# Attention output kept in channel layout: transposes replaced by a transfer between partitions, row sums spread as a factor, three near rows

## The reference, cut to what matters

```
logits = einsum('bqhgd,bqkhd->bqhgk', qg, k_sel) * HEAD_DIM**-0.5 + bias   # only selected keys
p = softmax(logits)
o = einsum('bqhgk,bqkhd->bqhgd', p, v_sel)
y_a = (o * silu(g_attn)) @ w_attn_out
```

## Time and profile before

| what | us |
|---|---|
| median of 3 runs | 3389.51 |
| lowest and highest run | 3388.55, 3389.98 |
| the profiled execution's own time | 3395.7 |
| its span, first to last instruction | 3394.0 |
| attention stage, first full step to last product | 894.9 |

### The profile page before, as it was taken

One profiled execution on the slowest core, in us unless ns is written; L12 is line 12 of the kernel. 1 busy time (PEld: TensorE's weight loads), 2 busy tenths in 40 slices (PEclk: granted clock), 3 DMA queues, 4 the chain that ended last, 5 costly groups with the idle time before them and its releaser, 6 DMA issues. The chain is left out here.

```text
span 3394.0 us, 50403 instructions
## 1 busy us (share of the span) xinstructions
PE 3245.1 (96%) x19461; PEld 2999.2 (88%) x19461; DVE 2697.9 (79%) x4071; ACT 1467.3 (43%) x1961; POOL 1038.4 (31%) x888
## 2 busy tenths in 40 slices
PE   7999999999999999999998999999999989899998
PEld 4999888999999999999997887787777879899987
DVE  2542788898989999999995999999999965875444
ACT  2322566988930200001002776676767740432121
POOL 3222111543335300000002453444533324674200
PEclk9999998999999999999998999999999999999999
DMA  6465535445555643344445323223222245577343
GB/s 236 131 190 165 155 100 141 158 149 187 185 180 178 256 177 138 138 162 170 159 144 145 78 59 81 75 57 99 59 60 61 60 154 199 159 236 257 127 143 114
DMA packets 381524, 485.53 MB, mean 143 GB/s; under 512 B 49296, under 2 KB 304464, under 8 KB 379685
## 3 DMA queue, kind: packets, MB, share of 16 engines
q1 hardware_dynamic: 325605, 287.14, 28.2%
q10 hardware_dynamic: 44352, 149.49, 12.4%
q0 software_dynamic: 11392, 46.68, 3.5%
HBM read 301.98 MB, written 184.13 MB: 143 GB/s over the span
## 5 line engine op out<-in xcount | busy, mean ns | idle before, releaser
L1140 PE MATMUL psum<-ha,gt 128*128 128x352 f32 x8136 | 1352.8, 324 | 7.7 <-DVE ha L1414 4.4
L1140 PEld LDWEIGHTS psum<-ha,gt 128*128 128x128 f32 x8136 | 1323.0, 189 | 11.6 <-DVE ha L1414 4.7
L1450 DVE SCALAR_TENSOR_TENSOR cv<-cv,vecs,cv 128x1056 f32<-128x1056 f32 (+1 forms) x480 | 607.7, 1342 | 0.0
L1942 ACT CAST at<-psum 128x1024 fp32r<-128x1024 f32 (+2 forms) x308 | 289.5, 940 | 265.2 <-PE psum L1853 263.4
L2016 DVE TENSOR_TENSOR at<-psum,at 128x1024 fp32r<-128x1024 f32 (+2 forms) x308 | 346.7, 1126 | 6.3 <-ACT at L1942 5.8
L717 PE MATMUL psum<-br,br 128*128 128x352 f32 x2016 | 337.1, 328 | 15.0 <-DVE br L2389 10.5
L1853 PE MATMUL psum<-ident,at 128*128 128x128 f32 (+1 forms) x2320 | 344.6, 272 | 6.0 <-DVE at L2016 4.8
L717 PEld LDWEIGHTS psum<-br,br 128*128 128x128 f32 x2016 | 330.4, 190 | 19.4 <-issue 11.8
L1271 ACT ACTIVATE gt<-psum 128x1056 f32<-128x1056 f32 x80 | 84.0, 1050 | 600.3 <-PE psum L1140 600.3
L791 DVE TENSOR_SCALAR_CACHE_REDUCE gl<-gt,gl 128x1792 bf16<-128x1792 f32 (+8 forms) x263 | 337.7, 1350 | 1.2
L1872 PE MATMUL psum<-at,at 128*128 128x512 f32 (+1 forms) x1160 | 327.2, 391 | 7.4 <-ACT at L1950 7.3
(11 more groups left out here) (255 smaller groups left out, 4142.7 us busy)
## 6 DMA issues: line engine op xcount, KB each, us to landing
scratch_ws<-gt SPq DMA_DIRECT2D x112, 512.0 KB, 4.0
gt<-scratch_ws ACTq DMA_DIRECT2D x110, 512.0 KB, 5.0
gt<-in_w_in_dram SPq DMA_DIRECT2D x60, 512.0 KB, 5.8
scratch_gm<-gt ACTq DMA_DIRECT2D x32, 528.0 KB, 3.0
br<-scratch_gm ACTq DMA_DIRECT2D x32, 528.0 KB, 3.7
scratch_m<-br POOLq DMA_DIRECT2D x32, 528.0 KB, 5.1
at<-scratch_q SPq DMA_DIRECT2D x128, 128.0 KB, 2.9
scratch_u<-gl POOLq DMA_DIRECT2D x16, 528.0 KB, 4.2
```

Of the source, the lines that this page charges most:

```text
L1140: return nc.tensor.matmul(of[:, j, 0:W // 3], part[:, c, :], a[:, c, j * (W // 3):(j + 1) * (W // 3)], start=(c == 0 and k == 0), stop=(c ...
L1450: ins = nc.vector.scalar_tensor_tensor(to[:, 0:width], mine[:, k_:k_ + width], tap, to[:, 0:width], ALU.mult, ALU.add)
L1942: nc.scalar.copy(phi[j % 3][:, 0:len(mine), 0:n], turned[j % 2][:, 0:len(mine), 0:n]).then_inc(s_phi, 1)
```

## The change

The output never leaves the channel layout. ScalarE copies the accumulator as before. A transfer brings the other 64 partitions beside the unit's own side (units alternate between the lower and the upper half), and GpSimd adds the two halves there (`fold`). The reciprocals of the row sums go out to memory as a row and come back broadcast to 64 partitions (`total_row`, `spread`); GpSimd multiplies them into the gate, reading them at a stride of four (`gain`). VectorE makes one multiplication of the two (`finish`), and SyncE stores from the accumulator's copy. TensorE's six transposes per unit and VectorE's three instructions are gone, and the ring holds score chunks alone. GpSimd walks the steps now, has three near rows instead of two (each with its mask part copied) and splits the queries of the next unit after the fourth near row; gates have four buffers.

```diff
+        self.total_at = at(self.first)
+        self.spread_at = at([n + 2 for n in self.first])
+        self.gain_at = at([n + 4 for n in self.first])
+        self.move_at = at([n + self.LAG + 1 for n in self.last])
+        self.fold_at = at([n + self.LAG + 2 for n in self.last])
+        self.out_at = at([n + self.LAG + 4 for n in self.last])
-        self.rows_at = at([n + self.LAG + 1 for n in self.last])
-        self.cols_at = at([n + self.LAG + 2 for n in self.last])
...
+        for e in range(GROUP * count):
+            self.near_at[ends[e - self.NEARS] if e >= self.NEARS else self.begin].append((e // GROUP, e % GROUP))
...
# SyncE
+            def total_row(u):
+                n = plan.queries(u)
+                sp.wait_ge(s_total, u + 1)
+                sp.dma_start(scr["ri"][u, 0:GROUP * n].rearrange("(q h) -> q h", h=GROUP), rinv[0:n, u % 4, :]).then_inc(s_row[u % 2], 16)
+            def move(u):
+                n = GROUP * plan.queries(u)
+                sp.wait_ge(s_acc, u + 1)
+                if u >= 2:
+                    sp.wait_ge(s_fold, u - 1)
+                sp.dma_start(moved[side(u), 0:n], accs[u % 2][side(u + 1), 0:n]).then_inc(s_move[u % 2], 16)
+            def spread(u):
+                n = GROUP * plan.queries(u)
+                sp.wait_ge(s_row[u % 2], 16 * (u // 2 + 1))
+                if u >= 2:
+                    sp.wait_ge(s_gain, u - 1)
+                sp.dma_start(wide[side(u), 0:n], scr["ri"][u:u + 1, 0:n].to_broadcast([HD, n])).then_inc(s_wide[u % 2], 16)
...
# GpSimd
+            def near_row(u, h):
...
+                if e >= plan.NEARS:
+                    pool.wait_ge(s_ring, plan.final(*divmod(e - plan.NEARS, GROUP)) + 1)
+                row = near[e % plan.NEARS]
+                if width > n:
+                    nc.gpsimd.tensor_copy(row[:, 0:width - n], mine[:, o:o + width - n])
+                nc.gpsimd.tensor_tensor(row[:, width - n:width], bias[g % 2][:, h, c0:c0 + n],
+                                        mine[:, o + width - n:o + width], ALU.add).then_inc(s_near, 1)
+            def settled(s, u, folds, gains):
+                if u % 2:
+                    pool.wait_ge(s_near, plan.nears_before[s])
+                    pool.wait_ge(s_query, 2 * min(plan.nears_before[s] // GROUP + 1, len(units)))
+                    pool.wait_ge(s_fold, folds)
+                    pool.wait_ge(s_gain, gains)
+            def gain(s, u):
+                n = plan.queries(u)
+                settled(s, u, plan.folds_by[s], u)
+                pool.wait_ge(s_ga[u % plan.GATES], 16 * (u // plan.GATES + 1))
+                pool.wait_ge(s_wide[u % 2], 16 * (u // 2 + 1))
+                nc.gpsimd.tensor_tensor(gate(u), gate(u), wide[side(u), 0:GROUP * n].rearrange("d (q h) -> d h q", h=GROUP),
+                                        ALU.mult).then_inc(s_gain, 1)
+            def fold(s, u):
+                n = GROUP * plan.queries(u)
+                settled(s, u, u, plan.gains_by[s - 1])
+                pool.wait_ge(s_move[u % 2], 16 * (u // 2 + 1))
+                nc.gpsimd.tensor_tensor(folded(u), folded(u), moved[side(u), 0:n], ALU.add).then_inc(s_fold, 1)
...
+            for s in plan.steps:
+                for u in plan.fold_at[s]:
+                    fold(s, u)
+                for u in plan.gain_at[s]:
+                    gain(s, u)
+                for u, h in plan.near_at[s]:
...
+                    near_row(u, h)
+                    if h == GROUP - 1 and u + 1 < len(units):
+                        queries(u + 1)
...
# ScalarE, ahead of the accumulator's copy
-                        act.wait_ge(s_rp, plan.slot[("rows", u - 2)] + 1)
+                        act.wait_ge(s_st[u % 2], 16 * (u // 2))
# VectorE (rows and columns removed here, as on TensorE)
+            def totals(u):
+                n = plan.queries(u)
+                dve.wait_ge(s_exp, GROUP * (u + 1))
...
+                nc.vector.reciprocal(rinv[0:n, u % 4, :], total[0:n, u % plan.SUMS, :]).then_inc(s_total, 1)
+            def finish(u):
+                dve.wait_ge(s_gain, u + 1)
+                dve.wait_ge(s_fold, u + 1)
+                mine = folded(u).rearrange("d (h t) -> d h t", h=GROUP)
+                nc.vector.tensor_tensor(mine, mine, gate(u), ALU.mult).then_inc(s_out, 1)
```

More of the change, by code:

```diff
@@ L1465 @@
     SUMS = 6
+    NEARS = 3
+    GATES = 4
     TILES = [t for k in range(NT // 2) for t in (k, NT - 1 - k)] + [NT]
@@ L1514, in __init__ @@
             seen += 1
-        self.end = len(self.pairs) + self.LAG + 4
+        self.end = len(self.pairs) + self.LAG + 5
         self.steps = range(self.begin, self.end)
@@ L1533, in __init__ @@
         for s in self.steps:
-            for key in ([("max",) + x for x in self.chunks_at[s]] + [("rows", u) for u in self.rows_at[s]]
-                        + [("cols", u) for u in self.cols_at[s]]):
-                self.slot[key] = len(self.slot)
+            for x in self.chunks_at[s]:
+                self.slot[("max",) + x] = len(self.slot)
     def queries(self, u):
@@ L1616, in attention_stage, with side, gate, folded @@
         block = ctx.enter_context(nc.Block())
+        def side(u):
+            return slice((u % 2) * HD, (u % 2 + 1) * HD)
+        def gate(u):
+            return ga[u // 2 % 2][side(u), :, 0:plan.queries(u)]
+        def folded(u):
+            return accs[u % 2][side(u), 0:GROUP * plan.queries(u)]
         def bank(key):
@@ L1715, in _ @@
                         queries(u)
+                for u in plan.move_at[s]:
+                    move(u)
+                for u in plan.spread_at[s]:
+                    spread(u)
+                for u in plan.total_at[s]:
+                    total_row(u)
                 for u in plan.store_at[s]:
@@ L1786, in nears @@
                 o = keys_of(t)[1] - width
[L1787 to L1800, removed]
@@ L1807, in _ @@
                               10: lambda g, k: keys_high(g, k, 1), 11: lambda g, k: keys_low(g, k, 1), 12: group_high}
-            for u in range(2, len(units)):
-                queries(u)
-                nears(u, parts_of_group.get(u % NTL) if u // NTL + 1 < KV else None)
+            queries(0)
+            for s in plan.steps:
[4 more added lines that the diff above has]
+                for u, h in plan.near_at[s]:
+                    if h == 2 and u % NTL in parts_of_group and u // NTL + 1 < KV:
+                        parts_of_group[u % NTL](u // NTL + 1, u % NTL)
+                    near_row(u, h)
+                    if h == GROUP - 1 and u + 1 < len(units):
+                        queries(u + 1)
+                        if u == 0:
+                            values_low(0)
@@ L1875, in values @@
                     last.then_inc(s_pv, 1)
[L1877 to L1893, removed]
             pe.wait_ge(s_set, SET)
@@ L1910, in _ @@
                     scores(*todo.pop(0))
[L1911 to L1914, removed]
         @block.scalar
@@ L1975, in masked @@
                     dve.wait_ge(s_near, GROUP * u + h + 1)
-                    other = near[h % 2][0:n, 0:w]
+                    other = near[(GROUP * u + h) % plan.NEARS][0:n, 0:w]
                 else:
@@ L2017, in _ @@
                                             phi[j % 3][:, 0:len(mine), 0:n].bitcast(F32), ALU.subtract).then_inc(s_plo, 1)
[L2018 to L2021, removed]
+                for u in plan.total_at[s]:
+                    totals(u)
+                for u in plan.out_at[s]:
+                    finish(u)
 def branch_stage(nc, mem, x, w, out, scr):
```

86 lines of the change are left out of this document (40 added, 46 removed).

## The result

The changed kernel takes 3344.0 us as the median of 4 runs (3341.4 to 3348.7), against 3389.7 before: a ratio of 0.9858, 95% interval 0.9841 to 0.9875. The forecast was 3343.

What follows compares the result with a forecast made beforehand. TensorE and VectorE, both nearly full, bound the 894.9 us attention stage. VectorE's 784 us plus 64 idle gives 848: -47, tail +0.5, so 3349 from the profiled 3395.7; runs' median 6.2 us lower: 3343. Range 3314 to 3372.

Steps and rivals of the forecast that it cites:

- Two engines side by side: Attention stage, 894.9 us: TensorE busy 851.4 and VectorE 830.9, each handing the other work in every step.
- The sum's last step: Stage time: of TensorE's count, 828 us, and VectorE's, 848 us, the larger governs, giving -47 us.
- VectorE's sum: VectorE's busy time in the attention stage: 830.9 - 110 + 63 = 784 us, plus 64 us idle.
- The part put on: New VectorE multiplication per unit: 0.688 us plus 0.27 us waiting for GpSimd, 63 us for the stage.
- the remark that most cases meet no wait: VectorE's multiplication at L1997 in the kernel before: its median, 0.426 us, shows most cases do not wait for GpSimd.
- TensorE's 48 us: Six transposes for each of 68 units leave TensorE, saving 48 us; 19.5 us of waits behind L1997 go too.
- The rival in which TensorE governs: Attention stage: VectorE's idle time shrinks as TensorE's work gets shorter, giving 3315 to 3323 us; chance 0.14.
- The near rows: GpSimd's row buffers in the attention stage: the third covers its new waits at fold time, a step and a half.
- The move: 128 KB SBUF-to-SBUF transfer before the fold: 0.36 + 2.3 = 2.7 us, just covered by a 2.9 us step.
- The sums' way: Row sums out to memory and broadcast back: two steps, 5.8 us, per leg; 16-byte pieces up to 6.6 us; cost zero.
- The blocked multiplication: Rival: the new VectorE multiplication waits out GpSimd instructions, 3370 to 3414 us, deciding from 1.62 us each; chance 0.09.
- The tail: End of the attention stage, last copy through fold and multiplication to last store: 0.5 us later.

Runs made afterwards that it cites:

- the dead loads: Changed kernel with work nobody reads put back per unit: six TensorE transposes (ratio 0.9922 to the kernel before), one 512-column VectorE reduction (0.9950), or both (0.9977).
- the run with both dead loads: Changed kernel with six unread TensorE transposes and one unread VectorE reduction per unit put back: ratio 0.9977 to the kernel before, 3381 us.
- the run without data: Kernel before, its two column transposes reading the identity without waiting for VectorE's scaled rows, all instructions kept: ratio 1.0001.
- the run that put them back: Changed kernel with unread transposes and reductions placed through the three-bank ring, two more ring turns per unit: ratio 0.9984 to the kernel before.

## Why the prediction was right

**Two engines side by side** was the right picture, and the dead loads show it: 22 us come back with TensorE's work, 31 with VectorE's, 40 with both. The sum's last step was not right: it took the larger of two counts, "the larger one governs", and in the runs neither count governs alone. Work on either engine is felt to some three quarters: 25.8 us of stage for 34.7 of TensorE's, 29.3 for 39.2 of VectorE's.

**VectorE's sum** came out at 791.7 us for 784, because the 110 us taken off were added up from durations, and neighbouring instructions overlap, as TensorE's do: in the timeline of the kernel before, a gate multiplication of 0.42 us begins at 2244.18 and the next instruction at 2244.51, 0.33 later. The part put on was sized well, and by its terms: 59.8 + 2.7 = 62.5 us for the forecast 63; 0.68 us without GpSimd for 0.688, and 0.25 us of standing behind it for 0.27. Only the remark that most cases meet no wait did not carry over: 49 of 64 begin inside an instruction of GpSimd, 17 of 64 before. VectorE's idle time fell to 52.8 us where the sum kept 64.0. The two errors, +8 and -11, nearly cancel; 848 against 844.5 is closer than its parts, and that closeness is luck.

**TensorE's 48 us** measured 42.4 of busy time. The 19.5 us of waits that its own count also took off did not leave so simply: TensorE's idle time fell by 8.0 us only, since 22.9 us of it now end with VectorE's masking and subtraction (4.8 us with the subtraction before). The rival in which TensorE governs rested on that step, and did not come about.

**The near rows** are where the prediction was right with too little said. It named the third row as the cover for GpSimd's waits and gave no price for the lack of it. The run with two rows puts it at 47 us, all of the gain, about a third of it as slower products. And the cover is just long enough: with the fold a step earlier, 23 us are lost. Alone in the kernel before the third row costs 10 us, so it is no gain of its own; it is what lets the rest through.

**The move** lands after 3.9 us, not 2.3. The sums' way makes 1.1 us of it, as the run without it shows; what makes the other 0.5 is not shown. Its price was taken from transfers over 128 partitions in emptier queues, and it differs from them in both. GpSimd stands at the fold 110 us, which the forecast called "just covered". It was harmless because of the rows, not because the transfer was in time.

**The sums' way** costs nothing, as forecast: in pieces of 16 bytes the row lands after 2.3 us. But the reason given for any landing up to 6.6 us left out what stands behind SyncE's wait: the moves. In the run with 4-byte pieces a wait of 5.3 us on average (300.5 / 57) comes through as 159 us in all. The landings there are later than 6.6 us (the broadcast is issued 8.9 us after its row at 2301.64, and 10.6 after the one at 2317.78), so what 6.6 would cost is not shown.

**The blocked multiplication** stayed a rival: far below the 1.62 us from which it would have decided. GpSimd's total was 622 us for 604; the strided gain costs 0.28 us more than one in order (1.567 against 1.284), inside the bounds and taken as nothing. A strided product well above 1.3 us was on the prediction's list of what would show it wrong; it came, and GpSimd had room for it. **The tail** grew by 1.4 us, not 0.5:

```profile
2709.05 0.37 ACT L2007 COPY at<-psum 128x256 f32<-128x256 f32 x1 [1.05 <-PE psum L1951]
2709.41 0.60 SPq L1745 DMA_DIRECT2D scratch_a<-at  x1
2710.10 0.57 SPq L1732 DMA_DIRECT2D at<-at  x1
2712.29 0.72 POOL L1870 TENSOR_TENSOR at<-at,at 64x256 f32<-64x256 f32 x1 [2.19 <-DMA at<-at]
...
2713.56 0.60 SPq L1745 DMA_DIRECT2D scratch_a<-at  x1
```

The last move goes out 0.7 us after the copy's end, behind the store of the unit before, and takes 2.2 us from then on.

What stays open: the last 8 us (0.0023 of 3390; 3 to 12 by the interval) between the run with both dead loads and the kernel before. The turns of the ring are argued for by the waits of the run without data, but the run that put them back doesn't tell. The waits of the run with both dead loads speak for another part, the query split, which the third near row lets GpSimd make earlier: TensorE waits 1.8 us for it (5.0 with the turns of the ring), 11.0 in the kernel before, while its waits behind VectorE (13.6, 5.5 and 4.9 us) add up to what they were before (11.1, 8.4 and 4.8). That is read from one execution of each, and no run tests it.

```profile
PE psum L1918 <- POOL at L1830: 1.8, 5, 0.5
```

The fourth gate buffer was not taken out by itself either. No version tried was clearly faster than the changed kernel.

## What to carry to other kernels

Where two engines are nearly full and hand work to each other, take work off both; here one half alone would have kept some 9 or 18 us of 40. When work moves to an engine that others wait for in order, look at what is queued behind its new waits, and give that queue one buffer more: here a third near row of 2 KB per partition decided between all and nothing. Count the engine's standing, not only its busy time.

## What the runs showed that was not expected

- One more buffer, in the kernel before, shifted GpSimd's query split and key preparation so that a VectorE instruction with two SBUF inputs stood longer behind them, 0.777 us on average for 0.581, and the kernel became 10 us slower. The added copies themselves stood in front of none of these.
- 68 small transfers of at most 2 KB, cut into 4-byte pieces instead of 16-byte ones, cost 159 us of a 3344 us kernel. SyncE, which issues them, stood 279 us longer before the broadcasts that need them.
- 128 KB transfers landed 0.6 to 0.7 us later (store 1.8 to 2.5, gate load 2.3 to 2.9) once they covered 64 partitions and the queues' share had gone from 25% to 39%, and the time didn't show it. Of the loads that kept their shape, the query load lost 0.2 us and the mask load of 256 KB 2.0 (2.6 to 4.6). No run separates share and shape.
- Where TensorE was kept waiting more, its clock fell too: with two near rows the same 4814 products took 15.0 us longer at a mean granted clock of 0.98, with the 4-byte pieces 55 us longer at 0.93.
